# The sum of fourteen experts added by VectorE alone, and three more chunks of weights loaded ahead

## What is computed

```python
# x: 512 latent tokens, ctx: 256 context tokens, D = 1024, 16 experts
x = x + mod_l[5] * expert_choice_ffn(h_lat, moe_router[i], moe_w_gate[i], moe_w_up[i], moe_w_down[i])
if not last:
    ctx = ctx + mod_c[5] * expert_choice_ffn(h_ctx, moe_router[i], ...)
```

## Time and profile before

| | us |
|---|---|
| median of 3 runs (lowest, highest) | 2898.89 (2898.24, 2905.34) |
| profiled execution: time | 2895.68 |
| profiled execution: span | 2893.8 |
| TensorE busy | 2568.2 (89%) |
| VectorE busy | 1199.8 (41%) |
| ScalarE busy | 417.1 (14%) |
| queue of SyncE (q1), share of the sixteen DMA engines | 49.2% |
| queue of POOL (q0) | 3.1% |
| queue of ScalarE (q10) | 0.9% |

### The profile page before, as it was taken

How to read it: one execution, slowest core, us unless ns; L and a number is a source line. 1 busy time by engine, 2 the same in 40 slices (tenths; PEclk the granted TensorE clock), 3 DMA queues, 4 the chain that set the end, 5 groups by cost and what they waited for, 6 DMA issues and landing times. The chain is left out here.

```text
span 2893.8 us, 52995 instructions
## 1 busy us (share of the span) xinstructions
PE 2568.2 (89%) x23739; PEld 1798.4 (62%) x23739; DVE 1199.8 (41%) x2046; ACT 417.1 (14%) x924; POOL 253.2 (9%) x227
## 2 busy tenths in 40 slices
PE   4999888679999998999788788888879988899999
PEld 2575674357888555578533564444438766788888
DVE  3736465521111112436767623222235555434552
ACT  2100451200000001100133200000010243110000
POOL 1000000122222210001100110000001300000000
PEclk8999988889999999899999889999999998999999
DMA  6431313589999994214343389999963200222211
GB/s 257 144 143 60 96 38 116 220 335 399 402 403 399 400 403 168 100 46 128 97 131 117 160 361 419 418 418 418 419 276 140 87 15 1 102 87 88 104 68 62
DMA packets 110906, 596.51 MB, mean 206 GB/s; under 512 B 13040, under 2 KB 35504, under 8 KB 47576
## 3 DMA queue, kind: packets, MB, share of 16 engines
q1 hardware_dynamic: 95304, 560.14, 49.2%
q0 software_dynamic: 12000, 22.48, 3.1%
q10 hardware_dynamic: 3376, 10.49, 0.9%
HBM read 572.77 MB, written 16.10 MB: 203 GB/s over the span
## 5 line engine op out<-in xcount | busy, mean ns | idle before, releaser
L1127 PE MATMUL moe_ps<-moe_ring,moe_xs 128*32 128x256 f32 x10240 | 597.5, 382 | 75.9 <-DMA moe_ring<-in_experts 60.8
L1127 PEld LDWEIGHTS moe_ps<-moe_ring,moe_xs 128*32 128x32 f32 x10240 | 388.1, 110 | 284.0 <-DMA moe_ring<-in_experts 84.1
L1127 PE MATMUL moe_ps<-moe_ring,moe_hid_t 128*32 128x256 f32 x5120 | 292.5, 380 | 11.5 <-DMA moe_ring<-in_experts 10.8
L1127 PEld LDWEIGHTS moe_ps<-moe_ring,moe_hid_t 128*32 128x32 f32 x5120 | 190.0, 110 | 114.4 <-DMA moe_ring<-in_experts 25.3
L1366 DVE TENSOR_TENSOR moe_hid<-moe_silu,moe_ps 128x512 f32<-128x512 f32 x32 | 22.0, 687 | 411.7 <-PE moe_ps L1127 411.7
L1327 DVE SCALAR_TENSOR_TENSOR x_feat<-moe_ps,mod,x_feat 128x512 f32<-128x512 f32 (+1 forms) x160 | 104.7, 718 | 120.9 <-PE moe_ps L1201 120.7
L1280 ACT ACTIVATE moe_silu<-moe_ps 128x512 f32<-128x512 f32 x32 | 19.1, 597 | 787.2 <-PE moe_ps L1127 787.2
L1390 DVE TENSOR_SCALAR moe_y<-moe_ps,moe_gates 128x256 f32<-128x256 f32 x42 | 17.7, 478 | 263.5 <-PE moe_ps L1127 263.5
L1158 POOL DMA_INDIRECT moe_rows<-h_rows,moe_rows_id x80 | 77.3, 966 | 472.8 <-DVE moe_xs L1347 363.2
L1168 POOL DMA_INDIRECT acc<-moe_y,moe_rows_id x42 | 66.7, 1588 | 348.4 <-DVE moe_y L1390 339.8
L590 PE MATMUL ffg_ps<-h_feat,feed_f_slots 128*128 128x256 f32 x352 | 81.9, 385 | 1.4 <-DVE h_feat L789 0.9
(11 more groups left out here) (682 smaller groups left out, 3901.4 us busy)
## 6 DMA issues: line engine op xcount, KB each, us to landing
moe_ring<-in_experts SPq DMA_DIRECT2D x384, 1024.0 KB, 27.7
x_feat<-in_ada_w SPq DMA_DIRECT2D x16, 1024.0 KB
feed_f_slots<-in_ffn_gate SPq DMA_DIRECT2D x11, 1024.0 KB, 4.8
feed_f_slots<-in_ffn_up SPq DMA_DIRECT2D x11, 1024.0 KB, 4.8
feed_f_slots<-in_ffn_down SPq DMA_DIRECT2D x8, 1408.0 KB, 6.8
mod_ada_w<-in_ada_w SPq DMA_DIRECT2D x2, 4096.0 KB, 14.4
qk_ada_w<-in_ada_w SPq DMA_DIRECT2D x8, 1024.0 KB, 4.8
gate_rows<-in_ada_w SPq DMA_DIRECT2D x8, 1024.0 KB, 5.0
```

The source lines that it names most:

```text
L1127: mm = pe.matmul(group_ps(part, g)[32 * q:32 * q + 32], turned[:, k * GROUP:(k + 1) * GROUP], ring[:, n % SLOTS, m, q * QUARTER:(q + 1) * ...
```

## The change

1. **Three guests.** After `h_turned` says that all of `K.h` is turned, SyncE loads chunks 12, 13 and 14 into `K.h`'s place, in both layers, still during the routing. From chunk 15 on the ring of 12 is used as before: chunks 15 to 26 take the slots of chunks 0 to 11, and chunk n from 27 on waits for chunk n - 12.
2. **The columns of the down matrices** of experts 0 to 13 in layer 0 are stored in another order (a reordering of the weights before the launch), so that a row of `acc` split in quarters turns by 32 x 32 blocks straight into the layout of `K.x`.
3. **`y` holds the factor too.** `mod[5]` is spread and turned once (`spread_gates`), and L1390's operation multiplies by the score and by it.
4. **The load of acc** goes to four DMAs of 32 partitions, in pieces of one quarter row (256 floats), issued by ScalarE before the last gate.
5. **VectorE adds the sum itself**: nine times a turn of up to three blocks and an addition to `K.x` (`add_sum`), four before the copy of expert 14's result, five after. It waits for the load first.
6. **TensorE no longer turns acc** (L1189 is gone) and does not wait for the load.

The diff, without the renamings that follow from it:

```diff
@@ route
                 prefetch(sp)
+                sp.wait_ge(sig["h_turned"], 2 * nt)
+                prefetch_into_h(sp)
@@ experts_stage
+        flat_h = K.h[:].rearrange("p k t -> p (k t)")
+        guests = [flat_h[:, n * 2 * D:(n + 1) * 2 * D].rearrange("p (m d) -> p m d", m=2) for n in range(3)]
+        AHEAD = SLOTS + len(guests)
+        def slot(n):
+            return n if n < AHEAD else (n - AHEAD) % SLOTS
+        def home(n):
+            return ring[:, slot(n)] if slot(n) < SLOTS else guests[slot(n) - SLOTS]
...
-            acc_tok = K.h[:].rearrange("p k t -> p (k t)")[:, 0:nt * D].rearrange("p (t c) -> p t c", c=D)
+            BLOCKS = nt * P // GROUP
+            acc = K.h[:].rearrange("p k t -> p (k t)")[:, 0:nt * D].rearrange("p (b c) -> p b c", c=QUARTER)
+            pieces = [(b, min(b + G, end)) for start, end in ((0, LT * 4), (LT * 4, BLOCKS)) for b in range(start, end, G)]
+            turned_acc = (y, rows)
+            shares = sbs("shares", [P, 2, QUARTER])
@@ sync
-                    for n in range(SLOTS, len(source)):
-                        sp.wait_ge(sig["w_used"], n - SLOTS + 1)
+                    for n in range(AHEAD, len(source)):
+                        last_user = n - AHEAD if n < AHEAD + SLOTS else n - SLOTS
+                        sp.wait_ge(sig["w_used"], last_user + 1)
                         load_chunk(sp, n)
@@ tensor
-                        if both:
-                            for u in batch:
-                                r, dt = units[u]
-                                t0, t1, _, _ = streams[r]
-                                for tt in range(t0, t1):
-                                    pe.matmul(ps[:, room(u), (tt - t0) * P:(tt - t0 + 1) * P],
-                                              acc_tok[:, tt, dt * P:(dt + 1) * P], K.ident[:], start=(tt == t0), stop=False,
-                                              skip_group_check=True)
...
-                    if both:
-                        pe.wait_ge(sig["sum_landed"], 16)
@@ scalar
+                    def load_sum():
+                        act.wait_ge(sig["added"], 16 * G * LATE)
+                        by_quarter = dram[f"acc{layer}"].rearrange("(b t a) c -> a t b c", t=GROUP, a=4)
+                        for a in range(4):
+                            act.dma_start(acc[32 * a:32 * a + 32], by_quarter[a]).then_inc(sig["sum_landed"], 16)
                     for e in range(LAST):
+                        if both and e == LATE:
+                            load_sum()
                         gate(e + 1)
...
-                    if both:
-                        act.wait_ge(sig["added"], 16 * G * LATE)
-                        act.dma_start(acc_tok, dram[f"acc{layer}"].rearrange("(t p a) c -> p t (a c)", p=P, a=4)
-                                      ).then_inc(sig["sum_landed"], 16)
@@ vector
+                    def add_sum(first, end):
+                        for n in range(first, end):
+                            b0, b1 = pieces[n]
+                            temp = turned_acc[n % 2][:, 0:b1 - b0]
+                            if n >= 2:
+                                dve.wait_ge(sig["acc_added"], n - 1)
+                            dve.transpose(temp.rearrange("p b c -> p (b c)"),
+                                          acc[:, b0:b1].rearrange("p b c -> p (b c)")).then_inc(sig["acc_turned"], 1)
+                            dve.wait_ge(sig["acc_turned"], n + 1)
+                            xv = K.x[:, :, b0 * GROUP:b1 * GROUP].rearrange("p k (b t) -> p k b t", t=GROUP)
+                            dve.tensor_tensor(xv, xv, temp.rearrange("p b (k t) -> p k b t", t=GROUP),
+                                              ALU.add).then_inc(sig["acc_added"], 1)
+                    def spread_gates():
+                        for r in range(2):
+                            wide = y[:, r].rearrange("p (k t) -> p k t", t=GROUP)
+                            dve.tensor_copy(wide, K.mod[:, layer, r, 5 * KT:6 * KT, 0].unsqueeze(2).to_broadcast([P, KT, GROUP])
+                                            ).then_inc(sig["gates_wide"], 1)
+                        dve.wait_ge(sig["gates_wide"], 2)
+                        dve.transpose(shares[:].rearrange("p r c -> p (r c)"),
+                                      y[:, 0:2].rearrange("p r c -> p (r c)")).then_inc(sig["shares"], 1)
+                        dve.wait_ge(sig["shares"], 1)
...
                         elif e == LATE:
+                            dve.wait_ge(sig["sum_landed"], 64)
+                            add_sum(0, 4)
                             dve.wait_ge(sig["w_used"], used_up(e, DOWN))
                             dve.tensor_copy(alone_y[:, 0, 0:2].rearrange("p g c -> p (g c)"), lat_ps(DOWN))
                             dve.tensor_copy(alone_y[:, 0, 2], ctx_ps(DOWN)).then_inc(sig["y"], 1)
+                            add_sum(4, len(pieces))
+                            dve.wait_ge(sig["acc_added"], len(pieces))
                         elif e < LATE:
...
-                                ins = dve.tensor_scalar(y[:, g], group_ps(DOWN, g), gates[:, g, e, :], None, ALU.mult)
+                                ins = dve.scalar_tensor_tensor(y[:, g], group_ps(DOWN, g), gates[:, g, e, :],
+                                                               shares[:, int(g == 2)], ALU.mult, ALU.mult)
@@ weights, before the launch
+        if layer == 0:
+            most = w[:EXPERTS - 2, 2].reshape(EXPERTS - 2, D, KT, 4, GROUP)
+            w[:EXPERTS - 2, 2] = most.transpose(0, 1, 3, 2, 4).reshape(EXPERTS - 2, D, D)
```

More of the change, by code:

```diff
@@ L893, in log_sigmoid_on_scalar, with route @@
     act.activation(y, y, ACT.Exp, scale=-1.0).then_inc(sig[key + "_exp"], 1)
-def route(nc, K, dram, layer, nt, streams, router, router_landed, ids, norm, prefetch):
+def route(nc, K, dram, layer, nt, streams, router, router_landed, ids, norm, prefetch, prefetch_into_h):
     name = f"route{layer}"
@@ L1091, in experts_stage @@
               {"rows": rows_id, "gates": gates, "place": place},
-              modulated_norm(K, layer, 1, segments), first_expert)
+              modulated_norm(K, layer, 1, segments), first_expert,
+              lambda sp: [load_chunk(sp, n) for n in range(SLOTS, AHEAD)])
         with ExitStack() as sub:
@@ L1120, in product @@
                     n = first_chunk[e, part] + c
-                    pe.wait_ge(landed[n % SLOTS], 16 * (n // SLOTS + 1))
+                    has_landed(pe, n)
+                    weights = home(n)
                     for m in range(2):
@@ L1127, in product @@
                                 mm = pe.matmul(group_ps(part, g)[32 * q:32 * q + 32], turned[:, k * GROUP:(k + 1) * GROUP],
-                                               ring[:, n % SLOTS, m, q * QUARTER:(q + 1) * QUARTER],
+                                               weights[:, m, q * QUARTER:(q + 1) * QUARTER],
                                                start=(k == 0 and g != 1), stop=(k == KT - 1), skip_group_check=True)
@@ L1183, in add_alone, with spread_result @@
                             pe.wait_ge(sig["alone_summed"], 4 * at)
-                        if both:
-                            for u in batch:
-                                r, dt = units[u]
-                                t0, t1, _, _ = streams[r]
-                                for tt in range(t0, t1):
-                                    pe.matmul(ps[:, room(u), (tt - t0) * P:(tt - t0 + 1) * P],
-                                              acc_tok[:, tt, dt * P:(dt + 1) * P], K.ident[:], start=(tt == t0), stop=False,
-                                              skip_group_check=True)
-                        spread_result(batch, alone_y[:, e % 2], e % 2, room, not both, "alone_turned")
-                    def spread_result(batch, result, which, place, begin, done):
+                        spread_result(batch, alone_y[:, e % 2], e % 2, room, "alone_turned")
+                    def spread_result(batch, result, which, place, done):
                         r = units[batch[0]][0]
@@ L1201, in spread_result @@
                                 mm = pe.matmul(ps[:, place(u), 0:span(u)], result[quad, g, (dt % 2) * P:(dt % 2 + 1) * P],
-                                               onehot[quad, which, g, 0:span(u)], start=(begin and g == groups[0]),
+                                               onehot[quad, which, g, 0:span(u)], start=(g == groups[0]),
                                                stop=(g == groups[-1]), skip_group_check=True)
@@ L1210, in add_last @@
                                 pe.wait_ge(sig["summed"], u - BANKS + 1)
-                        spread_result(batch, last_y, LAST % 2, bank, True, "turned")
+                        spread_result(batch, last_y, LAST % 2, bank, "turned")
                     def token_sums(batch):
@@ L1360, in _ @@
                         fill_onehot(LAST)
+                        spread_gates()
```

6 lines of the change are left out of this document (4 added, 2 removed).

## The result

| | before | after |
|---|---|---|
| median of 6 runs, us (lowest, highest) | 2901.19 (2898.24, 2905.34) | 2924.71 (2914.59, 2926.91) |
| profiled execution: time, us | 2895.68 | 2926.14 |
| profiled execution: span, us | 2893.8 | 2924.4 |

The ratio is 1.0074 (95% interval 1.0056 to 1.0092): slower, and beyond the 2917 at which the range ended. The forecast was 2906.

The account below looks back on a forecast made before the run. Layer 0 was bound by TensorE first, layer 1 by weights; +13.9 us in layer 0 and -7.0 in layer 1 made +6.9, 2902.6 us on the profiled execution; with the median 3.2 above, 2906, range 2881 to 2917.

Parts of the forecast that it names:

- How fast it comes: Layer 0's load of acc beside weights: 85 pairs at 0.33 + 0.045 us, then 107 pieces alone, 4.8 us.
- S: Time at which layer 0's load of acc has landed for VectorE, forecast at 1117 us.
- Turns one to one: While acc loads in layer 0, each engine alternates one weight packet with one 1 KB piece of ScalarE's queue.
- rival A: Layer 0's load faster, several pieces a turn: 2892 us at four, 2882 at eight; chance 0.28.
- Piece and packet: Prices during layer 0's load of acc: 0.33 us a weight packet, 0.045 a 1 KB piece.
- Rival B: Layer 0's load slower, pieces into 32 partitions up to 0.10 us: S = 1128, layer 0 +25, 2917 us; chance 0.12.
- Load start: ScalarE issues layer 0's load of acc at 1077.3 us; first packet 2 us later, at 1079.3.
- (15,UP) near 1104.7: Expert 15's up product in layer 0 ends near 1104.7 us instead of 1114.1, as TensorE loses weight waits.
- The tail: Layer 0 after S: hid_t at S + 19.8, then 19.1 us including 3.5 for the slow clock, end 1155.9.
- Layer 1 -7.0: Layer 1's expert stage: three prefetched chunks gain 7.5 us, less 0.5 for the first gather.
- about two 8 KB packets: What layer 1's first gather of rows waits for behind the prefetched chunks: 0.5 us.

## Why the prediction was wrong

The step that failed is the price of a packet and of a piece in "How fast it comes": 0.33 and 0.045 us, taken from loads over 128 partitions for a load over 32. From the first piece to the last the load took 48.4 us, where the sum has 85 x 0.375 + 107 x 0.045 = 36.7; that is 11.7 of the 14.9 us by which S came late.

- **Turns one to one**: right (768 to 766 packets), and with it the rejection of rival A, several pieces a turn. Equal counts alone would also fit several packets against several, but the starts of the pieces recur at 0.34 to 0.36 us in the single load over 128 partitions and at 0.40 to 0.42 us in the change, which is about one weight packet and one piece (0.364 and 0.425 by their prices). The 9 to 17 descriptors a packet of the Trainium skill ("DMA: Bandwidth & Descriptors", queues, rings and completion order) are not seen in these two loads.
- **Piece and packet**: wrong. 0.371 + 0.054 = 0.425 us a pair in place of 0.375, and 0.083 in place of 0.045 for the pieces alone. With the forecast's own counts these prices give 45.0 us; the rest of the 48.4 goes with the still dearer packets from 1113 us on. With 128 partitions the forecast's working is met: 36.8 us from the first piece to the last against 36.7, and 40.8 from issue against 39.7.
- **Rival B was the nearest**, at a chance of 0.12. It had 0.43 a pair, S = 1128 and +25 us in layer 0; on before's clock S was 1131.9, and the stage +24.7. Its condition was the right one, its split was not: it put the whole price on the piece (0.10 us) and left the weight packet at 0.33, where 0.054 and 0.371 were measured, so that its pair came out right is partly luck. I held 0.042 us from the earlier trace rows against it, though the prediction itself says that no row shows a load of 32 partitions: that row could not speak on the question. B's condition was a plain fact of the diff and only its price unknown, so it deserved a far larger share. From B's 2917 to the result it is layer 1 (3.3 us more), the median of before, 2901.19 over six runs and not 2898.89, and the scatter of unchanged code.
- **Load start**: issued at 1079.5 on before's clock, forecast 1077.3. The first gather of layer 0 is late there too (TensorE's wait 8.7 us, not 7.2), and from the last add to the load it took 12.3 us, not 11.8. From the issue to the first packet the sum allowed 2 us by estimate; it was 3.5 us in the change and 3.4 to 3.6 in the kernel before and in the loads of one DMA over 128 partitions and of 4 KB pieces. From the last packet to VectorE's first piece it was 0.5 us, where the sum had 1. So S was late by 2.2 + 1.5 + 11.7 - 0.5 = 14.9 us.
- **(15,UP) near 1104.7**: wrong, 1111.3 on before's clock. TensorE saved 2.9 us and not 9.4, because the dear packets delayed its weights (waits of 0.42 to 1.79 us from 1092 on; 5.9 us of them from 1073, and 1.4 in the same stretch with one DMA over 128 partitions) and the first gather came 1.5 us late. It cost nothing: VectorE was last by 29 us.
- **The tail**: right. hid_t at S + 18.4 (forecast S + 19.8), from there to the end of (15,DOWN) 16.3 us (19.1). The clock did drop to 0.50, but only 1.7 and 1.9 us were lost to it, the first of them under VectorE's work. Together: S 14.9 us late, 4.2 us less behind it, 10.8 us over the forecast.
- **Layer 1 -7.0**: it was -3.7. The mis-sized term is the gather's "about two 8 KB packets": 3.5 us and not 0.5. The saving of 7.5 us was not measured by itself: TensorE's waits for weights fell by 5.7 us in the change and by 7.7 with the guests alone, and guests behind the gather gained 4.5, not 7. So what is open is how much three chunks are worth there.
- **ScalarE's issue**: not in the prediction at all. Nothing hung on it in the change; it would have been the next bound by 4 us.

Sum: 10.8 in layer 0 and 3.3 in layer 1 are 14.1 us over the forecast of +6.9, which gives the 21.0 of the two stages.

## What to carry to other kernels

Before a transfer is cut into one DMA for each quadrant to get a layout for free, price it as a different kind of load: here each filled 32 partitions, and it slowed the weight stream of another queue as much as itself. Put a wait for a long load behind everything that does not need it on that engine, and look at which queue issues it, for an issue can block the queue. And count what a large prefetch costs a small transfer issued behind it: here 3.5 us at the start of a stage. Issuing the prefetch second brought the small one back, but gained nothing that the runs can tell from issuing it first.

## What the runs showed of the hardware

- A load over 32 partitions makes the packets of both queues dearer: 8 KB weight packets took 0.371 and 0.491 us instead of 0.317 while its pieces of 1 KB and 4 KB ran beside them. Where each queue had about half of the engines' time, an 8 KB packet took 0.54 us beside pieces into 32 partitions and 0.32 beside pieces into 128, and a piece 0.087 and 0.050.
- ScalarE's queue was blocked by issues: four DMAs of 768 pieces took 34.38 us in all, 32.86 of them the fourth (28.71 in all over 128 partitions), four of 192 pieces 1.82 us, a single one of 3072 pieces 0.38 us. What limit lies behind it stays open.
- A gather issued behind three queued chunks reached TensorE 3.5 us later than without them, more than the two packets that I had counted; its first packet started 4.2 us after the issue and not 1.7.
- The DMA share falls to one half well before the load is in (53.1% from 1132 to 1138 us), as in the earlier trace rows; the records of the single transfers have 8 to 9 packets in flight there and 16 to 17 before 1118 us. So half of the engines lag. Why, no run was made to tell.
